# The delta rule's raw k turned by DMA and 32x32 block transposes instead of TensorE, with inverse and scan moved to later slots

## The reference

```python
h = x @ w_in[l]
dq, dk, dv, dz, db, da, aq, ak, av, ga, gb = split(h)
o_a = gated_deltanet(dq, dk, dv, dz, db, da, ...)
o_b = diff_attention(aq, ak, av, ...)
merged = sigmoid(ga) * (o_a @ w_branch_a) + sigmoid(gb) * (o_b @ w_branch_b)
x = layer_norm(ALPHA * x + merged @ w_out)
x = layer_norm(ALPHA * x + (silu(x @ w_gate) * (x @ w_up)) @ w_down)
```

## Time and profile before

| | us |
|---|---|
| median of 3 runs | 1892.54 (1891.83 to 1893.61) |
| the profiled execution | 1892.05 |
| its span, first to last instruction | 1889.9 |
| TensorE (PE) busy | 1876.0 |
| VectorE (DVE) busy | 1322.6 |
| ScalarE (ACT) busy | 919.6 |
| GpSimd (POOL) busy | 184.7 |

### The profile page before, as it was taken

How to read it: one execution, slowest core, us unless ns; L and a number is a source line. 1 busy time by engine, 2 the same in 40 slices (tenths; PEclk the granted TensorE clock), 3 DMA queues, 4 the chain that set the end, 5 groups by cost and what they waited for, 6 DMA issues and landing times.

```text
span 1889.9 us, 29981 instructions
## 1 busy us (share of the span) xinstructions
PE 1876.0 (99%) x9647; PEld 1548.7 (82%) x9647; DVE 1322.6 (70%) x1859; ACT 919.6 (49%) x1234; POOL 184.7 (10%) x448
## 2 busy tenths in 40 slices
PE   9999999999999999999999999999999999999997
PEld 7888888878888888888888887888888888888886
DVE  7878888888676767675677657577775466654656
ACT  5656565664455555556444447444443444443442
POOL 0202020020023233333000000000000000000000
PEclk9999999999999999999999999999999999999999
DMA  7667666575567776776665775566666666665565
GB/s 276 220 202 223 204 214 225 188 242 166 189 198 240 219 245 214 241 222 209 203 193 195 233 237 169 199 189 195 193 196 194 191 192 197 191 196 192 190 192 175
DMA packets 121041, 389.69 MB, mean 206 GB/s; under 512 B 14512, under 2 KB 27632, under 8 KB 120816
## 3 DMA queue, kind: packets, MB, share of 16 engines
q1 hardware_dynamic: 97904, 351.65, 58.2%
q10 hardware_dynamic: 19200, 28.34, 4.9%
q0 software_dynamic: 3840, 8.39, 1.6%
HBM read 368.91 MB, written 19.42 MB: 205 GB/s over the span
## 4 chain that ended last, share of the span: by engine, by line
PE 97%; DVE 1%; DMA 0%; issue 0%; ACT 0%; SPq 0%; DVEq 0%; ACTq 0%
PE pg L496 92%; PE B L496 5%; DVE gates L1474 1%; DMA raw<-in_weights 0%; PE B L596 0%; ACT whi L870 0%; PE B L816 0%; DVE wlo L1466 0%; DVE act_b L1466 0%; PE B L744 0%; DVE lnst L2170 0%; DVE sm L1474 0%; DVE act_a L1466 0%; DVE lnst L2175 0%; ACT L1390 0%
## 5 line engine op out<-in xcount | busy, mean ns | idle before, releaser
L1466 DVE TENSOR_TENSOR wlo<-raw,whi 128x1024 fp32r<-128x1024 f32 (+1 forms) x640 | 778.6, 1219 | 472.8 <-ACT whi L870 454.2
L870 ACT ACTIVATE whi<-raw 128x1024 fp32r<-128x1024 f32 (+1 forms) x640 | 674.3, 1057 | 751.8 <-PE pg L496 706.2
L496 PE MATMUL pg<-whi,act_x 128*128 128x512 f32 x2960 | 936.2, 393 | 1.0 <-ACT whi L870 1.0
L496 PEld LDWEIGHTS pg<-whi,act_x 128*128 128x128 f32 x2960 | 555.6, 188 | 120.2 <-issue 3.7
L496 PE MATMUL pg<-wlo,act_x 128*128 128x512 f32 x1480 | 574.7, 390 | 0.0
L496 PE MATMUL pg<-whi,act_a 128*128 128x512 f32 x1632 | 504.7, 389 | 0.1
L496 PEld LDWEIGHTS pg<-whi,act_a 128*128 128x128 f32 x1632 | 306.3, 188 | 64.2 <-DVE act_a L1466 0.8
L496 PEld LDWEIGHTS pg<-wlo,act_x 128*128 128x128 f32 x1480 | 278.1, 188 | 54.9
L496 PE MATMUL pg<-wlo,act_a 128*128 128x512 f32 x816 | 317.5, 389 | 0.0
L496 PEld LDWEIGHTS pg<-wlo,act_a 128*128 128x128 f32 x816 | 153.2, 188 | 31.7
L496 PE MATMUL pg<-whi,act_b 128*128 128x512 f32 x512 | 158.4, 389 | 0.0
(11 more groups left out here) (264 smaller groups left out, 1067.8 us busy)
## 6 DMA issues: line engine op xcount, KB each, us to landing
raw<-in_weights SPq DMA_DIRECT2D x646, 512.0 KB, 4.3
turn_c<-hraw ACTq DMA_DIRECT2D x8, 512.0 KB, 3.3
qT<-turn_c ACTq DMA_DIRECT2D x32, 128.0 KB, 4.5
turn_q<-hraw ACTq DMA_DIRECT2D x6, 512.0 KB, 4.5
gates<-turn_q ACTq DMA_DIRECT2D x24, 128.0 KB, 4.6
turn_p<-gates POOLq DMA_DIRECT2D x12, 192.0 KB, 3.4
gates<-turn_p POOLq DMA_DIRECT2D x48, 48.0 KB, 4.0
decm<-sums_out ACTq DMA_DIRECT2D x4, 512.0 KB, 3.9
```

What stands on the lines that cost most here:

```text
L496: return nc.tensor.matmul(o, l, r, start=start, stop=stop)
L870: return nc.scalar.activation(o, i, ACT.Copy, scale=scale)
L1466: return V.tensor_tensor(o, a, b, op)
```

## The change

It does six things, all in the delta rule:

- k is copied to `hraw` in blocks, written to `turn_c`, read back in four transfers and turned by VectorE, as v and q are; `dn_conv` of TensorE and its semaphore are gone, and the taps of k read `rawT`. The counts of the semaphores `c_kept`, `c_full` and `dve_raw` go from two to three a body.
- k is read back in slot 10 and turned in slot 11; its convolution moves from slots 8 and 10 to 12 and 13, its SiLU from 11 to 14. v is turned in slot 20 instead of 21, its convolution moves from 22 and 23 to 21 and 26, its SiLU from 24 to 27.
- The inverse moves three slots later: the product k with k from 13 to 16, norms from 14 and 15 to 17 and 18, the inverse of blocks of 32 from 19 to 22, growing steps to 24 to 26, `OFF_P` to 28, `OFF_T` to 30, `OFF_COPY` to 29. The blocks of v are written from slot 28 on instead of 25.
- `OFF_64` becomes a function of its own, `dn_join`, and runs in slots 0 and 1 of the next body.
- The scan moves two slots later: k with q from slot 0 to 2, the rest from 1 to 3 on; scaling and blocks of o from 11 and 12 to 13 and 14; O_HI from 18 to 20.
- The decays move two slots later (`sums_in` from 2 to 4, Relus from 5 to 8 to 7 to 10), the masks too.

```diff
-CONV_SLOTS = [(8, 10), (22, 23), (29, 30)]
-RAW_SLOTS = (21, 28)
+CONV_SLOTS = [(12, 13), (21, 26), (29, 30)]
+RAW_SLOTS = (11, 20, 28)
...
-OT_SLOTS = (12, 14)
-O_SCALED, O_BLOCKS, V_BLOCKS = 11, 12, 25
-C_BACK, K_BLOCKS, K_BACK, K_TAIL, AT_SCALED = (18, 25), 17, 22, 26, (19, 20)
-O_HI, O_LO = 18, (26, 27)
-MASK = (17, 18)
-SCAN = 1
+OT_SLOTS = (14, 16)
+O_SCALED, O_BLOCKS, V_BLOCKS = 13, 14, 28
+PROD, NORM, INVERSE = 16, 17, 22
+C_BACK, K_BLOCKS, K_BACK, K_TAIL, AT_SCALED = (10, 18, 25), 19, 22, 27, (21, 22)
+O_HI, O_LO = 20, (26, 27)
+MASK = (19, 20)
+SCAN = 3
...
-DECAY = range(5, 9)
+DECAY = range(7, 11)
...
-GROW = {21: 0, 22: 1, 23: 2}
+GROW = {24: 0, 25: 1, 26: 2}
-OFF_P, OFF_T, OFF_COPY, OFF_64 = 25, 27, 26, 29
+OFF_P, OFF_T, OFF_COPY, OFF_64 = 28, 30, 29, 0
...
         def conv_in(kind, h):
-            if kind:
-                return rawT[:, h, :]
-            return B[h // 2][:, h % 2 * SEQ:(h % 2 + 1) * SEQ]
+            return rawT[:, h, :]
...
-            def dn_conv(j, s):
-                if s not in CONV_SLOTS[0]:
-                    return
-                half = CONV_SLOTS[0].index(s)
-                pe.wait_ge(evac[0], 2 * j + 1)
-                if half == 0 and j:
-                    pe.wait_ge(N["dve_o1"], 1 + j)
-                for i in range(2):
-                    for t in range(TOK):
-                        h = 2 * half + i
-                        last = nc.tensor.transpose(conv_in(0, h)[:, t * P:(t + 1) * P],
-                                                   hraw[:, t, h * P:(h + 1) * P], ident)
-                last.then_inc(N["pe_conv"], 1)
...
-                if i == 0:
-                    if not isinstance(j, int):
-                        act.wait_ge(c_kept, 32 * j)
-                    rows_out(0, lambda t: hraw[:, t, :])
-                elif i < 3:
-                    if i == 1:
-                        act.wait_ge(N["pe_conv"], 1 + 2 * (j + 1))
-                    else:
-                        act.wait_ge(c_kept, 16 * (2 * j + 1))
-                    if i == 2 or not isinstance(j, int):
-                        act.wait_ge(c_full, 64 * (2 * j + i - 1))
+                if i < 3:
+                    if i or not isinstance(j, int):
+                        act.wait_ge(c_kept, 16 * (3 * j + i))
+                        act.wait_ge(c_full, 64 * (3 * j + i))
...
                 if s in C_BACK:
                     i = C_BACK.index(s)
-                    act.wait_ge(c_kept, 16 * (2 * j + i + 1))
-                    act.wait_ge(N["dve_raw"], 1 + 2 * j + i)
+                    act.wait_ge(c_kept, 16 * (3 * j + i + 1))
+                    act.wait_ge(N["dve_raw"], 1 + 3 * j + i)
                     blocks_in(turn_c, moved, c_full)
...
                 if s in RAW_SLOTS:
                     i = RAW_SLOTS.index(s)
-                    dve.wait_ge(c_full, 64 * (2 * j + i + 1))
-                    dve.wait_ge(N["act_tap"], 1 + 6 * j + 2 * (i + 1))
+                    dve.wait_ge(c_full, 64 * (3 * j + i + 1))
+                    dve.wait_ge(N["act_tap"], 1 + 6 * j + 2 * i)
```

More of the change, by code:

```diff
@@ L354, in build @@
             dve_lnT dve_x1 pe_x1T x1f act_x1T dve_x1T pe_y act_gc pe_gT act_gT act_var dve_var act_root act_sig act_xn pro_chain ln_chain""".split()
-        counted = """pe_conv dve_raw dve_conv act_silu dve_cw act_tap
+        counted = """dve_raw dve_conv act_silu dve_cw act_tap
             dve_g act_past act_decay act_at dve_kS dve_ktail pe_kk dve_at dve_t act_tt dve_a8 pool_t8 dve_x pe_x pe_p dve_p pe_t
@@ L607, in dn_build @@
             def dn_build(j, s):
-                if s == 13:
+                if s == PROD:
                     pe.wait_ge(N["act_silu"], 1 + 3 * j + 1)
@@ L643, in dn_build, with dn_join @@
                     last.then_inc(N["pe_t"], 1)
+            def dn_join(j, s):
                 if s == OFF_64:
@@ L660, in dn_scan @@
             def dn_scan(j, s, alone=False):
-                if s == 0:
+                if s == SCAN - 1:
                     pe.wait_ge(N["act_silu"], 1 + 3 * j + 3)
@@ L762, in _ @@
                 mm(B[3][:, :], warm[:, 0:P], warm[:, 0:NG])
-            body(0, 0, act_x, [prologue, lambda s: dn_conv(0, s), lambda s: dn_build(0, s)], x_ready)
+            body(0, 0, act_x, [prologue, lambda s: dn_build(0, s)], x_ready)
             for j in range(1, NB):
-                body(j * BODY, 2 * j, act_x, [lambda s: dn_scan(j - 1, s), lambda s: dn_conv(j, s),
+                body(j * BODY, 2 * j, act_x, [lambda s: dn_join(j - 1, s), lambda s: dn_scan(j - 1, s),
                                               lambda s: dn_build(j, s)])
-            body(N_DA, 2 * NB, act_x, [lambda s: dn_scan(NB - 1, s, True)])
+            body(N_DA, 2 * NB, act_x, [lambda s: dn_join(NB - 1, s), lambda s: dn_scan(NB - 1, s, True)])
             with pe.Fori(1, NB) as j:
@@ L978, in dn_evac @@
                     last.then_inc(evac[i % 2], 1)
-                    act.wait_ge(evac[i % 2], 2 * j + i)
+                    act.wait_ge(evac[i % 2], 2 * j + max(i, 1))
                     act.dma_start(turn_c.rearrange("a x b c -> (a x) (b c)"), flat(hraw[:, :, :])).then_inc(c_kept, 16)
@@ L988, in dn_conv @@
                         half = slots.index(s)
[L989 to L992, removed]
+                        act.wait_ge(N["dve_raw"], 1 + 3 * j + kind + 1)
                         if half == 0:
@@ L1024, in dn_build @@
             def dn_build(j, s):
-                if s == 2 and not isinstance(j, int):
+                if s == SCAN + 1 and not isinstance(j, int):
                     sums_in(j)
@@ L1041, in dn_build @@
                         last.then_inc(N["act_at"], 1)
-                if s == 24:
+                if s == CONV_SLOTS[1][1] + 1:
                     silu(j, 1)
@@ L1136, in _ @@
             with act.Fori(1, NB) as j:
-                body(BODY * j, lambda n, i: dn_evac(n, i, j), [lambda s: dn_scan(j - 1, s), lambda s: dn_conv(j, s),
+                body(BODY * j, lambda n, i: dn_evac(n, i, j), [lambda s: dn_join(j - 1, s), lambda s: dn_scan(j - 1, s), lambda s: dn_conv(j, s),
                                                                lambda s: dn_build(j, s), lambda s: k_moves(j, s), lambda s: v_moves(j, s),
@@ L1148, in da_evac @@
                 if first and what == "q":
-                    act.wait_ge(c_kept, 32 * NB)
+                    act.wait_ge(c_kept, 48 * NB)
                     rows_out(i % 2, lambda t: hraw[:, t, :], scale=CH ** -0.5)
@@ L1243, in _ @@
             body(N_DA, lambda n, i: da_evac(n, i, 0, True),
-                 [lambda s: dn_scan(NB - 1, s, True)])
+                 [lambda s: dn_join(NB - 1, s), lambda s: dn_scan(NB - 1, s, True)])
             body(N_DA + BODY, lambda n, i: da_evac(n, i, 1, False), [lambda s: da_mix(0, s), lambda s: qk_back(1, s)])
@@ L1627, in dn_build @@
                     ch(V.tensor_copy(cur[:, :].unsqueeze(1), scal[:, bass.ds(j, 1), 0:NCUR]))
-                if s == 1 and not isinstance(j, int):
+                if s == SCAN and not isinstance(j, int):
                     g_next(j)
-                if s == 14:
+                if s == NORM:
                     dve.wait_ge(N["act_decay"], 1 + j + 1)
@@ L1643, in dn_build @@
                     ch(V.tensor_reduce(d_("ss"), Pc[:, :, :], X, ALU.add))
-                if s == 15:
+                if s == NORM + 1:
                     ch(ts(d_("ss"), d_("ss"), RMS_EPS, ALU.add))
@@ L1664, in dn_build @@
                     V.tensor_copy(t8, eye8.rearrange("p (r c) -> p r c", c=EB)).then_inc(N["dve_a8"], 1)
-                if s == 19:
+                if s == INVERSE:
                     dve.wait_ge(N["pool_t8"], 1 + j + 1)
@@ L1715, in dn_scan @@
                         v_scaled(j, t)
-                if s == 1:
+                if s == SCAN:
                     for t in range(TOK):
```

## The result

The changed kernel takes 1926.95 us in the median of four runs (1925.04 to 1931.58), the kernel before 1892.68: ratio 1.0186, 95% interval 1.0174 to 1.0199. That is 34.3 us slower; the forecast was 20 us slower (1912.0), and the result lies 2 us above its outer range (1894 to 1925). The profiled execution was the slowest of the four: 1931.58 us (span 1929.5), 39.5 us above that of before.

A forecast was written before the change was run, and what follows sets the result against it. TensorE, 97% of the chain, was taken as the bound. Waits of 6.2 us in each of three bodies and 5.0 in the first, less 3.6 of removed transposes, gave +20.0 us: 1912.0 us, range 1894 to 1925.

The forecast's parts named there:

- k's set in: Middle body: k's four read-backs, issued from 39.8 us, take 6.9 and are complete at 46.7 us (44.2 to 49.4).
- from norms to inverse: VectorE starts norms at 64.6 us; v's transpose and first convolution half lengthen the stretch from 18.6 to 20.4 us.
- inverse at 86.7: Middle body: inverse done at 85.0 us, TensorE wants it at 80.2, so it is 4.8 us behind in all.
- join's second product: Start of the next body: TensorE waits 1.4 us behind ScalarE's SiLU, z copy, rounding and join copies.
- The gain of 3.6: TensorE loses eight groups of k transposes at 0.45 us each, all on the path: 3.6 us saved.
- the k product: Middle body: SiLU ends at 57.9 us, TensorE wants k at 56.6 and stands 1.3 us, included in the 4.8.
- The first body's: First body: no o to scale or turn, Relus between k's taps; waits of 5.0 us, nothing at the join.
- the sum: Whole run: 6.2 us in each of three bodies plus 5.0 in the first, less 3.6: +20.0 us.
- the lower bound: All sets landing in 4.4 us: some 2.9 us a body at the inverse, nothing at the join: +8 us.
- rival (b): Short landings, no k wait, but the norms-to-inverse stretch starts late: +4 to +12 us, 1900 in the middle; chance 0.17.
- Rival (a): Everything stays hidden: k lands within about 4.4 us and only the removed groups count: -3.6 us, 1888.5; chance 0.15.
- an estimate of 3.7 us: k's read-backs by the skill's transfer rule: set in 3.7 us after first issue, before VectorE asks, leaving only +8.

The follow-up runs named there:

- run 1: The changed kernel with k still transposed by TensorE (slots 8 and 10), all other moves kept and no k transfers: 1909.97 us, ratio 1.0089.
- run 9: Kernel of run 1 with TensorE's k transposes and k's first taps in slots 12 and 13 instead of 8 and 10: 1918.65 us, ratio 1.0136.
- run 5: The kernel before with TensorE's transposes of k left out in bodies 1 to 3, nothing moved or transferred: 1889.0 us, ratio 0.9982.
- Run 2: The changed kernel without k's write-out and read-backs or the waits for them; VectorE turns whatever the buffer holds: 1916.80 us, ratio 1.0122.
- run 6: Kernel of run 1 with the join in slots 1 and 2 of the next body instead of 0 and 1: 1899.27 us, ratio 1.0036.
- run 11: Kernel of run 4 (later join) with k's read-backs issued in slot 9 instead of 10: 1913.67 us, ratio 1.0110.
- run 8: The kernel before with VectorE making the remainders of three output-projection tiles 6, 8 and 10 times over, so TensorE waits: 1914.35 us, ratio 1.0115.
- run 4: The changed kernel with the join in slots 1 and 2 instead of 0 and 1: 1914.85 us, ratio 1.0119.
- run 7: Kernel of run 4 with the growing steps and their sum also one slot later, the inverse staying in slot 22: 1918.33 us, ratio 1.0124.

## Why the prediction was right and wrong

**Right.** Direction, and much of the path in body 3: k's set in at 46.8 (46.7 predicted), norms at 65.0 (64.6), 20.6 us from norms to inverse in runs 1 and 9 (20.4), inverse at 86.7 (85.0; 1.4 us of it are the wait for v's read-backs), join's second product waiting 1.9 us (1.4) behind SiLU, z copy and rounding. Body 3 has 2.3 us at the first growing step, 1.8 at remainders and 1.9 at the join: 6.0 us, where I had 6.2. In the whole run the new waits are 32.6 - 2.7 = 29.9 us; without the 7.3 of "issue" 22.6, where I had 23.6. The gain of 3.6 holds within its interval (run 5).

**Part of the agreement is luck.** k's read-backs were issued at t = 41.2 and not 39.8, and the set took 5.5 us and not 6.9: two errors of 1.4 us that cancel. In the three middle bodies the waits outside the join are 3.6, 3.7 and 4.1 us, where I had 4.8 in each, and the k product, for which I had 1.3 us, waits 0.4, 0.5 and nothing. Against this the joins wait 1.3 us after the first body, where I had none, and 1.3, 1.9 and 1.9 after the others, where I had 1.4. The first body's 5.2 us (5.0 predicted) hold the 2.5 us at a remainder that I had not seen.

**The step that failed is the sum.** It added waits and a gain, and took TensorE at full clock for all work between the waits. The clock was no term in it at all: 9.9 us in the profiled run; the mean clocks of the four executions (0.993 to 0.995, before 0.998) give an estimate of 6 to 10. The second omitted term is "issue", 7.3 us: TensorE stands with no semaphore outstanding. The longest, 3.8 us, is in the middle of a growing step of body 1 (timeline, TensorE):

```profile
212.47 0.70 PE L495 MATMUL B<-Pm,Pc 32*32 32x32 f32 x58
217.00 0.32 PE L495 MATMUL B<-Pm,Pc 32*32 32x32 f32 x6 [3.83 <-issue]
```

One packet of an instruction queue moved in that time, so instructions that come late may be the cause; but both kernels have 63 such packets in the run, the kernel before has no such wait, and no run tested it. The cause stays open. 20.0 + 9.9 + 7.3 - 1.0 (waits fewer than forecast) = 36.2 of the 39.5 us by which the two profiled executions differ. Most of the other 3.3 is in TensorE's busy time and not in further waits: that rose by 9.4 us (1876.0 to 1885.4), and 9.9 - 3.6 = 6.3 of them are in the sum.

**Also wrong: the lower bound and rival (b).** I let the loss fall to +8 with fast landings and gave the join no wait then. Run 2 has no landings of k to wait for and loses 24.3 us. In it the join waits 7.4 us and the inverse's product 8.2; neither asks when k lands. The join's wait goes with its slot (run 6), the inverse's comes with the slots of k's taps (run 9). I gave the late set as the cause of late norms; runs 2 and 9 show the same wait with no set. The landings cost their 10 us beside it. Rival (a), all hidden, failed at the same two places.

**Landings.** In body 3 of the changed kernel k's set was in 5.5 us after its first issue, in run 11 it took 8.6. By the Trainium skill's page "DMA: Bandwidth & Descriptors" (anatomy of one DMA) an estimate of 3.7 us had stood beside the forecast; the trace disagrees with it here, as the earlier trace rows had. The Trainium skill's "VectorE: DVE Perf Modes" (rules for kernel authors) prefers TensorE for 128x128 transposes. The runs bear it out only in part: k's transfers alone cost 10.1 us for 3.6 us of transposes, but 17.4 of the 34.3 us came with moves that left the transposes on TensorE (run 1).

## What to carry to other kernels

When TensorE is 97% of the chain, count the clock with the waits: where bunches of waits of about 2 us appear, the run can lose more than their sum (12.1 us for a join that waited 6.4), and by an amount that differs between executions. A step moved by n slots does not take its cover along: price each wait again in the new order, and expect a wait that an in-order VectorE cannot absorb to reappear at the next step when you move the work in front of it. 3.6 us of matmuls are not worth work on queues that have less slack than that in each body.

## What the runs showed of the hardware

- The granted clock fell to 0.5 while TensorE stood still for 5.5 and 8.4 us in an otherwise full stretch, and it was low for 6.8 and 10.2 us, of which 3.7 and 4.3 us were work; a lone wait of 1.9 us brought no fall (run 8). In run 1 it did fall after a wait of 1.9 us. In the changed kernel it fell six times for 3.4 us, among waits of about 2 us; in run 4 the same waits of the first body (2.3 and 2.0 us) brought no fall, where the changed kernel's (2.5 and 2.0) brought one each.
- The same four 128 KB read-backs took 8.6 us instead of 5.5 when they were issued 4.7 us behind the issue of their write-out and not 6.9 (body 3); in body 1, 9.6 instead of 6.5. Counted from the write-out's issue they were in after 13.3 and 14.2 us, and in the changed kernel after 12.5 and 13.3: the earlier issue gained nothing there.
- TensorE's "issue" waits, one of 3.8 us in the middle of 64 products of 32x32 (7.3 us in the changed kernel, 3.5, 2.0, 5.5 and 6.1 in runs 2, 4, 11 and 7), were absent before. Their cause is not shown.
